# Hybrid encoder layer on one core: the second norm's shift and scale computed by VectorE as row products instead of by TensorE

## The reference, cut to what matters

```python
c_act = silu(c)                                   # c: (1, 1024)
mod = c_act @ ada_w + ada_b                       # ada_w: (1024, 6144), 24 MB
sh1, sc1, gt1, sh2, sc2, gt2 = split(mod, 6)
h = rms_norm(x, norm1_g) * (1 + sc1) + sh1
q, k, v, g_out, gk_low, z, xbc, dt_raw, gates = split(h @ w_in)
o_a = gla_mixer(q, k, v, g_out, gk_low, ...)      # linear attention
o_b = ssd_mixer(z, xbc, dt_raw, ...)              # causal convolution of xbc, state space
gate_a, gate_b = split(sigmoid(gates), 2)
x = x + gt1 * ((gate_a * (o_a @ w_oa) + gate_b * (o_b @ w_ob)) @ w_out)
h = rms_norm(x, norm2_g) * (1 + sc2) + sh2
x = x + gt2 * hier_moe(h, ...)                    # 32 experts, 2 per token, 3 MB of weights each
out = rms_norm(x, final_norm_g)
```

## Time and profile before

| what | value |
|---|---|
| median of 3 runs | 708.6 us |
| span of the profiled execution, first to last instruction | 709.2 us |
| PE busy | 683.8 us (96%) |
| DVE, ACT, POOL busy | 398.5, 258.5, 70.8 us |
| bytes moved by DMA | 200.76 MB |
| chain of waits | PE 78%, DMA 9%, SPq 5%, DVE 4%, ACT 2%, issue 2% |

### The profile page before, as it was taken

One profiled execution on the slowest core, in us unless ns is written; L12 is line 12 of the kernel. 1 busy time (PEld: TensorE's weight loads), 2 busy tenths in 40 slices (PEclk: granted clock), 3 DMA queues, 4 the chain that ended last, 5 costly groups with the idle time before them and its releaser, 6 DMA issues.

```text
span 709.2 us, 13401 instructions
## 1 busy us (share of the span) xinstructions
PE 683.8 (96%) x5734; PEld 552.0 (78%) x5734; DVE 398.5 (56%) x684; ACT 258.5 (36%) x365; POOL 70.8 (10%) x69
## 2 busy tenths in 40 slices
PE   8998999999999999999999999999999999999893
PEld 8898999999878777899989998766666666665441
DVE  3567677985785687987857467454324122221226
ACT  2344454547474442435544333232131221221003
POOL 0010000000000814400000000001112111111111
PEclk9999999999999999999999999999999999999997
DMA  9989677655435433336568658989999999999982
GB/s 366 414 310 374 247 269 272 245 176 187 165 119 178 172 126 119 119 120 238 179 238 286 241 202 312 372 293 392 419 376 420 420 420 421 418 419 419 419 340 100
DMA packets 31054, 200.76 MB, mean 283 GB/s; under 512 B 5031, under 2 KB 5415, under 8 KB 7826
## 3 DMA queue, kind: packets, MB, share of 16 engines
q1 hardware_dynamic: 27378, 193.27, 70.9%
q0 software_dynamic: 3616, 6.62, 2.6%
HBM read 194.83 MB, written 10.75 MB: 290 GB/s over the span
## 4 chain that ended last, share of the span: by engine, by line
PE 78%; DMA 9%; SPq 5%; DVE 4%; ACT 2%; issue 2%; DVEq 0%; ACTq 0%
PE ps L1487 76%; SPq L449 4%; DMA ring<-in_expert_pieces 4%; DMA r_kq<-in_pieces 3%; DVE ring_rounded L895 2%; DMA ring<-in_pieces 2%; ACT ring_rounded L613 1%; PE ps L1599 1%; PE ps L1903 1%; SPq L446 0%; DVE r_lm L1036 0%; DVE r_kq L1107 0%; DVE r_xs_rounded L1163 0%; ACT r_lm L707 0%; DVE r_kq L1101 0%
## 5 line engine op out<-in xcount | busy, mean ns | idle before, releaser
L895 DVE TENSOR_TENSOR ring_rounded<-ring,ring_rounded 128x2048 fp32r<-128x2048 f32 x60 | 138.2, 2308 | 70.0 <-ACT ring_rounded L613 69.8
L1487 PE MATMUL ps<-hT_rounded,ring_rounded 128*128 128x256 f32 x832 | 155.1, 286 | 2.0 <-DVE ring_rounded L895 2.0
L1487 PEld LDWEIGHTS ps<-hT_rounded,ring_rounded 128*128 128x128 f32 x832 | 131.9, 193 | 4.7 <-issue 4.7
L613 ACT CAST ring_rounded<-ring 128x2048 fp32r<-128x2048 f32 x60 | 114.2, 1905 | 55.4 <-PE ps L1487 27.9
L1487 PE MATMUL ps<-x_sb_rounded,ring_rounded 128*128 128x256 f32 x416 | 118.4, 285 | 0.0
L1487 PE MATMUL ps<-ring_rounded,hT_rounded 128*128 128x512 f32 x352 | 109.5, 392 | 0.0
L1487 PEld LDWEIGHTS ps<-x_sb_rounded,ring_rounded 128*128 128x128 f32 x416 | 80.4, 193 | 0.3 <-issue 0.2
L1487 PEld LDWEIGHTS ps<-ring_rounded,hT_rounded 128*128 128x128 f32 x352 | 65.3, 188 | 14.9 <-issue 1.7
L572 POOL DMA_INDIRECT y_rows<-r_st,r_btm x29 | 28.4, 981 | 348.6 <-DVE r_st L1370 348.6
L819 ACT ACTIVATE sq<-ps 128x128 f32<-128x128 f32 x32 | 8.9, 277 | 142.5 <-PE ps L1487 142.5
L1487 PE MATMUL ps<-ring,r_lm 128*64 128x256 f32 x512 | 59.2, 380 | 1.2 <-DMA ring<-in_expert_pieces 1.2
(11 more groups left out here) (324 smaller groups left out, 1019.3 us busy)
## 6 DMA issues: line engine op xcount, KB each, us to landing
ring<-in_pieces SPq DMA_DIRECT2D x74, 1024.0 KB, 5.0
ring<-in_expert_pieces SPq DMA_DIRECT2D x48, 1024.0 KB, 18.9
r_z<-in_expert_pieces SPq DMA_DIRECT2D x12, 1024.0 KB, 12.6
r_xs<-in_expert_pieces SPq DMA_DIRECT2D x12, 1024.0 KB, 14.2
g_sb<-in_expert_pieces SPq DMA_DIRECT2D x6, 1024.0 KB, 13.0
r_st<-in_expert_pieces SPq DMA_DIRECT2D x6, 1024.0 KB, 14.4
r_bt<-in_expert_pieces SPq DMA_DIRECT2D x6, 1024.0 KB, 18.4
hT<-in_expert_pieces SPq DMA_DIRECT2D x6, 1024.0 KB, 17.6
```

The costliest lines, as they stand in the source:

```text
L613: nc.scalar.copy(high_of(p_), slot_of(p_)).then_inc(hi_ok, 1)
L895: nc.vector.tensor_tensor(low_of(p_), slot_of(p_), high_of(p_).bitcast(F32), ALU.subtract).then_inc(lo_ok, 1)
L1487: return nc.tensor.matmul(o, l, r, start=start, stop=stop)
```

## The change

Modulation blocks 6 to 9 leave TensorE. Their weights come as eight pieces of a new kind, `row` (6,0) to (9,1), each of 256 columns of ada_w, laid out transposed: a column of ada_w is now a run of 1024 floats on one partition, two such runs a partition. silu(c) is laid out as a row of 1024 on every partition (`c_rows`, in r_pv): GpSimd loads it when the gate rows `gtb` have been made, ScalarE applies silu after the last gate. VectorE multiplies each run with `c_rows` and sums it in the same instruction (`accum_out`), two instructions a piece (`next_rows`), which gives two columns of `mod`; after the eighth piece it adds the bias and forms the scale. The row pieces stand in `PIECES` behind oa 0, oa 1, ob 0 and ob 1, two each.

```diff
-ADA_AFTER = {("xbc", i): 4 + i for i in range(6)}
+ADA_AFTER = {("xbc", i): 4 + i for i in range(2)}
+ROWS_AFTER = {("oa", 0): 6, ("oa", 1): 7, ("ob", 0): 8, ("ob", 1): 9}
...
-BLOCKS += [(_n, i) for _n in ("z", "gate") for i in range(4)]
-BLOCKS += [(_n, i) for _n in ("oa", "ob", "out") for i in range(2)]
+for _b in [(_n, i) for _n in ("z", "gate") for i in range(4)] + [(_n, i) for _n in ("oa", "ob", "out") for i in range(2)]:
+    BLOCKS += [_b] + ([("row", ROWS_AFTER[_b])] if _b in ROWS_AFTER else [])
...
+            elif kind == "row":
+                eng.wait_ge(row_read, ROW_PIECES.index(p_) + 1)
...
+            mix_wait(pool, ("gtb", 0, 1))
+            pool.dma_start(c_rows, c_row.partition_broadcast(P)).then_inc(s_crow, 16)
...
+                if i == 3:
+                    act.wait_ge(s_crow, 16)
+                    nc.scalar.activation(c_rows, c_rows, ACT.Silu).then_inc(crow_ok, 1)
...
-            link(nc.vector.scalar_tensor_tensor(mod[:, 32:40], mod[:, 32:40], 1.0, col("norm2", 0, 8), ALU.add, ALU.mult))
+            def next_rows():
+
+                n_r = next(row_pieces)
+                p_ = ROW_PIECES[n_r]
+                loaded(dve, p_)
+                dve.wait_ge(crow_ok, 1)
+                rows_ = slot_of(p_).rearrange("p a b -> p (a b)").rearrange("p (m k) -> p m k", m=2)
+                for m in range(2):
+                    at = 4 * p_[1] + 2 * p_[2] + m
+                    ins = nc.vector.scalar_tensor_tensor(rows_[:, m], rows_[:, m], 1.0, c_rows, ALU.mult, ALU.mult,
+                                                         accum_out=mod[:, at:at + 1])
+                ins.then_inc(row_read, 1)
...
                 ins.then_inc(mix_used(("obT", i)), 1)
+            next_rows()
+            next_rows()
...
                         ins.then_inc(unit_used((name, i), h), 1)
                         unit_taken(dve, (name, i), h)
+                        if (name, i) != ("ob", 1):
+                            next_rows()
+            dve.wait_ge(row_read, len(ROW_PIECES))
+            link(nc.vector.tensor_tensor(mod[:, 24:40], mod[:, 24:40], col("ada_b", 24, 16), ALU.add))
+            link(nc.vector.scalar_tensor_tensor(mod[:, 32:40], mod[:, 32:40], 1.0, col("norm2", 0, 8), ALU.add, ALU.mult))
```

More of the change, by code:

```diff
@@ L58 @@
 NCOL = PAR["ident"][0]
-ADA_AFTER = {("xbc", i): 4 + i for i in range(6)}
+ADA_AFTER = {("xbc", i): 4 + i for i in range(2)}
+ROWS_AFTER = {("oa", 0): 6, ("oa", 1): 7, ("ob", 0): 8, ("ob", 1): 9}
 ADA_FIRST = [2, 0, 3, 1]
-ADA_ORDER = ADA_FIRST + list(range(4, 10))
+ADA_ORDER = ADA_FIRST + [4, 5]
 BLOCKS = []
@@ L77 @@
 EARLY = [("ada", i, h, 0) for i in ADA_FIRST for h in range(2)]
-SPLITS = [p_ for p_ in PIECES if p_[0] not in ("ada", "gt")]
+SPLITS = [p_ for p_ in PIECES if p_[0] not in ("ada", "gt", "row")]
 SPLIT_AT = {p_: i for i, p_ in enumerate(SPLITS)}
-UNITS = [b_ for b_ in BLOCKS if b_[0] != "ada"]
+UNITS = [b_ for b_ in BLOCKS if b_[0] not in ("ada", "row")]
 TOKEN_MAJOR = ("k", "v", "g", "z", "out")
+ROW_PIECES = [p_ for p_ in PIECES if p_[0] == "row"]
 HALVES = [p_ for p_ in SPLITS if p_[0] in TOKEN_MAJOR and p_[2] == 0]
@@ L136, with trunk @@
     AHEAD_OF[_n] = AHEAD_IN_CONV if _at <= 12 else AHEAD
-def trunk(nc, x, final_norm_g, x_t, params, pieces, small_w, gk2_rows, router_w, gate_bias, expert_pieces, out):
+def trunk(nc, x, final_norm_g, x_t, params, pieces, small_w, gk2_rows, router_w, gate_bias, c_row, expert_pieces, out):
     with ExitStack() as ctx:
@@ L220, in trunk @@
         m_tmp = r_pv[:, 2, :]
+        c_rows = r_pv[:, 0:2, :].rearrange("p a b -> p (a b)")
         h2_parts = rounded["r_ct"][:].rearrange("p (t d) -> p t d", t=TT), rounded["r_v"][:].rearrange(
@@ L322, in trunk @@
             sem(n) for n in "late_ok late_turned late_back late_sum vals_ok gk_tm_ok".split())
+        s_crow, row_read, crow_ok = (sem(n) for n in "s_crow row_read crow_ok".split())
         y_two_ok = [sem(f"y_two_ok{i}") for i in range(2 * TT)]
@@ L1133, in _ @@
                 ins.then_inc(mix_used(("oaT", i)), 1)
-            link(nc.vector.scalar_tensor_tensor(mod[:, 32:40], mod[:, 32:40], 1.0, col("norm2", 0, 8), ALU.add, ALU.mult))
+            def next_rows():
[9 more added lines that the diff above has]
+                ins.then_inc(row_read, 1)
+            row_pieces = iter(range(len(ROW_PIECES)))
             def modulation_rows(w):
@@ L2023, in packed @@
     for n, (kind, i, h, r) in enumerate(EARLY + PIECES):
-        w, at = (of[kind], 0) if kind in of else (w_in, OFF[kind])
-        if kind == "gt":
+        w, at = (of[kind], 0) if kind in of else (w_in, OFF.get(kind, 0))
+        if kind == "row":
+            at = i * CW + h * HC
+            pieces[n] = by_partition(inputs["ada_w"][0][:, at:at + HC].T).reshape(P, KD, HC)
+        elif kind == "gt":
             pieces[n] = by_partition(of["ada"][i * D // 4:(i + 1) * D // 4, 10 * CW:12 * CW]).reshape(P, KD, HC)
@@ L2064, in packed @@
             "router_w": np.concatenate([by_partition(router).reshape(P, -1), router_b], axis=1),
-            "gate_bias": inputs["ada_b"][0][10 * CW:12 * CW].reshape(2, CW), "expert_pieces": experts}
+            "gate_bias": inputs["ada_b"][0][10 * CW:12 * CW].reshape(2, CW), "c_row": inputs["c"][0], "expert_pieces": experts}
 def kernel(**inputs):
```

## The result

The changed kernel takes 762.9 us (median of 4 runs, 760.75 to 764.68) against 708.65: 1.0765 of the time before, 95% interval 1.0742 to 1.0788. It is 54 us slower; 760 was forecast, in a range of 744 to 776. The profiled execution spans 760.5 us, against 709.2.

What follows compares the result with a forecast made beforehand. TensorE's progress before the expert stage was taken as the bound, the stage itself by bytes. Waits of 52.5 us, 59.3 with the clock, less 7.6 for the removal gave +51.7 us: 760 us, range 744 to 776.

Steps and rivals of the forecast that it cites:

- Removal: Four modulation blocks leave TensorE in the convolution, where VectorE keeps up: the full 7.6 us is gained.
- Points 1 to 3: From obT to the low part of ob(0,0,r=1), held behind row (8,0): TensorE 22.3 us late in all.
- point 1: At obT: oa(1,1) gets the slot of oa(0,0), so obT's low parts start 1.9 us late.
- point 2: ob(0,0,r=0) gets its slot only when row (6,1) has been read: TensorE stands for 5 us.
- Point 4: Row (8,1) takes the slot of ob(0,0,r=0), free two quarters later: TensorE 6.8 us idle, awaiting ob(0,1,r=0)'s low part.
- Point 5: Row (9,0) stands in SyncE's list behind ob(1,1,r=0), which waits for a slot: 14.7 us idle before ob(1,0).
- Point 6: Row (9,1) takes the slot of ob(1,0,r=0), free after three quarters: 6.9 us idle before ob(1,1).
- Clock: TensorE runs at half clock after each of four long waits, 1.7 us lost each time.
- Point 7: At out 0: out(0,1) waits for ob(1,1,r=0), so its low part comes 1.8 us late.
- slow product: Rival: a row product on VectorE takes 2.4 us, as a scaled reduction, giving 774 us; chance 0.11.
- Waits absorbed: Rival: after ob(0,0), TensorE's lateness gives later loads the time they lack; +16 us, 725; chance 0.07.
- faster: Rival: VectorE's 20 us of products fit in its idle time, no low part is late; 701 us; chance 0.05.

Runs made afterwards that it cites:

- 6: Changed kernel with row pieces moved from the ring into four empty expert slots, low parts first and pairs later; 700.9 us.
- 7: As 6, but VectorE takes each pair of products ahead of the next half's low parts, as in the changed kernel; 700.4 us.
- experiment 5: Changed kernel, but from ob(0,0) on VectorE splits the next half's pieces before each row pair, except row (9,1); 733.3 us.
- experiment 9: Changed kernel plus dummy products on TensorE (25, 46, 28, 58 and 25) ahead of five late pieces; 758.7 us.
- experiment 3: Changed kernel without the products: row pieces are loaded and waited for, a copy of one column stands for each pair; 750.0 us.
- experiment 4: As experiment 3, with each row piece's transfer cut from 1 MB to 64 KB; 735.5 us.
- experiment 8: Changed kernel plus dummy products on TensorE (30, 100, 45, 100 and 45) ahead of five late pieces; 776.8 us.

## Why the prediction was right

The mechanism and the number were both right, and the sum can be held against the trace term by term. That it met the number within 3 us is in part luck, since two errors of 2 to 3 us cancelled (the sum, below). What is measured below is idle time in the changed kernel's profile, or half of a stretch at half clock, unless it says otherwise.

- **Removal, 7.6.** The load that SyncE issues at 337.14 us before is issued at 327.08 after, 10.1 us earlier. Of that some 2.4 us are not the change's: in this execution TensorE's stop of the earlier trace rows was 1.31 us instead of 1.98 and the clock did not fall behind it. In the profiles of the experiments, with the same early part, the stop was 1.08 to 2.27 us. The rest is 7.7.
- **Points 1 to 3, 22.3 late.** The stop before obT grew from 0.61 to 2.68 us, 2.1 for the 1.9 of point 1; 6.11 for the 5 of point 2; then 11.30, and 2.75 of the clock. Together 22.2. The 11.30 lies under the 13 to 15 that were to show it, and with the 2.75 inside them. Row (8,0) was multiplied from 394.73; the prediction had it landed at 404.9 on the clock of the kernel before, less 10.1 = 394.8.
- **Point 4, 6.8:** 7.1. **Point 5, 14.7:** 14.5. **Point 6, 6.9:** 6.9.
- **Clock, 6.8:** 8.65 in the last four stretches. This term was too small: I took 3.5 us at half clock from the one example, and two of the stretches were 4.4 and 5.8 us long. The fall behind the first stop I had not charged at all; it lies inside point 3.
- **Point 7, 1.8:** 2.9. The load that waits for ob(1,1,r=0) was 49.1 us late (476.83 against 427.73), the first expert load 52.0, and 2.9 is the difference; 0.95 and 1.04 of it are idle time of TensorE in out 0.
- The sum: 22.2 + 7.1 + 14.5 + 6.9 + 8.65 + 2.9 = 62.3 against 59.3, less 10.1 = 52.2 against 51.7. The 3 us too few for the clock and point 7 met a removal that this pair of profiles shows 2.4 us too large.
- **The row product.** 1.22 us plus 0.08 for the sum, and a pair takes 2.38 us from start to end where I took 2.6. The slow product (2.4 us, 774) is refuted. With the sum 1024 floats took 1.22 us, as without. So the prediction's reading of the Trainium skill (Vector Engine (DVE) Microarchitecture Reference, "Points that are easy to get wrong"), by which two f32 sources in SBUF would double the time once a sum is wanted, is refuted for this form. The page doesn't say against what the half is measured, and no run here has bf16 sources. (The prediction's sum for that case is 776 and not 775: six pairs, 2.64 us longer each.)
- **Waits absorbed, 725, and faster, 701.** Both fell, by the stops at points 4 to 6. But "faster" named the right condition: VectorE's 20 us do fit, and 700.9 us is what the whole computation takes once no row piece is waited for (6 and 7).
- **Who ended the waits.** The prediction wanted a DMA named in front of four pairs; the profile names it for two, and the landing times show it for the others.
- **The hidden parts** stayed hidden. ScalarE's silu (1.06 us) and its table load (1.28 us) stand beside full TensorE work.

What I had not seen is what the waits consist of. I described them as pairs ahead of low parts, and expected experiment 5 to cure most of it. It gave back 29.6 of the 63 us over the removal alone. The ring has a large part in the rest: a row piece takes a slot out of five, and with it the lead of the weight behind it, and it is itself loaded late for the same reason. The two were not priced fully apart, since experiment 5 left row (9,1) and the first pairs in their places. The sum was right all the same, because it was made from issue times in SyncE's list, which hold both effects.

## What to carry to other kernels

Before adding an operand that is loaded late, write down for each of its loads which slot it takes, who frees that slot, and what stands behind it in the issuer's list; bandwidth and engine capacity (here both ample) do not answer that. Give such an operand buffers of its own that stand empty at the time, and its place before or behind the other work matters little (700.4 against 700.9 us here); in a shared ring it also shortens the lead of everything behind it. If the end of a stage hangs on slots, the time can be summed from issue times, and each stop should be charged with the clock behind it.

## What the hardware showed

- TensorE's granted clock stood at 0.50 for 3.4 to 5.8 us after each of the five long stops of the changed kernel, and the length doesn't follow that of the stop (3.4 after 14.54, 5.8 after 11.30). It was also at the lower level after a stop of 3.03 us in experiment 9, and full after ones of 2.68 us (before obT, changed kernel) and 2.65 us (experiment 3, ob(0,0)).
- Around 66 us, at one and the same place, it fell after stops of 1.84 us (experiment 9), 1.98 (before) and 2.27 (experiment 5), and stayed at 1.00 after 1.31 (after), 1.72 (experiment 3) and 2.09 us (experiment 4). Before obT it fell after 2.42, 2.44 and 2.49 us (experiments 3, 5 and 9) and stayed after 2.55 and 2.68 (experiment 4 and the changed kernel). The length of the stop alone doesn't decide. The stretch of experiment 4 (the columns as above, TensorE alone; the first 0.23 us of it are the end of the stop), against 0.51 in the earlier trace rows:

```profile
66.40:69.90 3.50, 3.27 (x27) 1.00 0.97 372
```

- A product of two 128x1024 f32 tiles with an accumulated sum took 1.22 us on VectorE, and reading the sum 0.08 us.
- The stop near 66 us was 1.08 to 2.27 us long from one profile to the next with the same instructions up to there. With the fall of the clock behind some of them, SyncE's load of 327.08 us in the changed kernel was issued between 326.78 (experiment 8) and 329.66 (experiment 5): 2.9 us between profiles, which no edit made.
